# A third weight slot, deeper norm buffers, ScalarE stores and a one-piece RWKV recurrence with four-tile updates

## What is computed

```python
def _wkv_step(S, inp):
    r_t, w_t, k_t, v_t, a_t, b_t = inp
    sa = jnp.einsum('zbhvk,zbhk->zbhv', S, a_t)
    S = S * w_t[..., None, :] + sa[..., :, None] * b_t[..., None, :] + v_t[..., :, None] * k_t[..., None, :]
    return S, jnp.einsum('zbhvk,zbhk->zbhv', S, r_t)
...
    def expert_block(args):
        xb, e = args
        return (jax.nn.silu(xb @ w_gate[e]) * (xb @ w_up[e])) @ w_down[e]
...
        hl2 = rmsnorm(x, norm2_g[i]) * (1 + sc2) + sh2
```

## Time and profile before

| | us |
|---|---|
| median of 3 runs | 4429.95 |
| profiled execution | 4436.23 |
| its span | 4434.4 |
| gMLP mixer | 0 to 657 |
| norm, routing, experts of layer 0 | 671 to 1334 |
| recurrence with its preparation | 1816 to 2725 |
| norm, routing, experts of layer 1 | 2839 to 3482 |
| rest of the layers | to 4434 |

### The profile page before, as it was taken

How to read it: one execution, slowest core, us unless ns; L and a number is a source line. 1 busy time by engine, 2 the same in 40 slices (tenths; PEclk the granted TensorE clock), 3 DMA queues, 4 the chain that set the end, 5 groups by cost and what they waited for, 6 DMA issues and landing times. The chain is left out here.

```text
span 4434.4 us, 104053 instructions
## 1 busy us (share of the span) xinstructions
PE 3704.5 (84%) x46088; PEld 2369.3 (53%) x46088; DVE 1252.4 (28%) x2933; ACT 775.7 (17%) x1775; POOL 620.5 (14%) x794
## 2 busy tenths in 40 slices
PE   4999995999992399688888886789999469997887
PEld 2445544555551145477777784456565234664464
DVE  2140114111110620245555554421111120331153
ACT  1011001000000100233433331100000010321142
POOL 0000000211110100244444430011111100000000
PEclk7999996999996599799999997789999779658988
DMA  7731105999996512100000003479999732101000
GB/s 277 286 146 38 72 19 193 394 396 384 388 392 222 130 69 76 50 15 17 18 18 18 17 6 112 145 284 397 392 388 386 257 98 90 38 1 63 24 39 24
DMA packets 303038, 707.10 MB, mean 159 GB/s; under 512 B 26829, under 2 KB 50349, under 8 KB 301964
## 3 DMA queue, kind: packets, MB, share of 16 engines
q1 hardware_dynamic: 268036, 613.55, 37.5%
q0 software_dynamic: 25840, 71.67, 4.8%
q10 hardware_dynamic: 8728, 15.34, 0.9%
HBM read 648.20 MB, written 52.31 MB: 158 GB/s over the span
## 5 line engine op out<-in xcount | busy, mean ns | idle before, releaser
L901 PE MATMUL banks<-w_gate_up_ring,x_turned 128*32 128x256 f32 x12288 | 695.3, 382 | 33.4 <-DMA w_gate_up_ring<-in_moe_w_up_dram 31.9
L901 PEld LDWEIGHTS banks<-w_gate_up_ring,x_turned 128*32 128x32 f32 x12288 | 425.8, 110 | 275.6 <-issue 56.6
L919 PE MATMUL banks<-w_down_ring,hidden_turned 128*32 128x256 f32 x6144 | 344.8, 380 | 0.0
L878 POOL DMA_DIRECT2D y_rows<-y_out_rows x256 | 142.0, 562 | 946.1 <-ACT y_out_rows L963 910.9
L977 DVE TENSOR_TENSOR hidden<-silu_gate,banks 128x128 f32<-128x128 f32 x192 | 55.3, 288 | 770.1 <-ACT silu_gate L957 770.1
L337 PE MATMUL banks<-const_cols,h_tokens 128*128 128x128 f32 x240 | 55.1, 411 | 250.0 <-DVE h_tokens L310 163.2
L919 PEld LDWEIGHTS banks<-w_down_ring,hidden_turned 128*32 128x32 f32 x6144 | 193.1, 110 | 128.6
L1914 DVE TENSOR_TENSOR inverse_both_ways<-banks,inverse_both_ways 128x512 f32<-128x512 f32 (+1 forms) x240 | 152.2, 637 | 253.2 <-PE banks L1823 252.3
L866 POOL DMA_INDIRECT x_rows<-h_rows,cell_index x64 | 62.9, 983 | 921.0 <-POOLq L42 895.4
L456 PE MATMUL banks<-gmlp_weights,h_turned_gmlp 128*128 128x512 f32 x384 | 174.7, 610 | 12.3 <-DMA gmlp_weights<-in_ga_w_in_dram 12.3
L337 PEld LDWEIGHTS banks<-const_cols,h_tokens 128*128 128x128 f32 x240 | 46.4, 220 | 259.5 <-DVE h_tokens L310 170.8
(11 more groups left out here) (456 smaller groups left out, 5475.4 us busy)
## 6 DMA issues: line engine op xcount, KB each, us to landing
w_gate_up_ring<-in_moe_w_gate_dram SPq DMA_DIRECT2D x70, 2048.0 KB, 19.8
w_gate_up_ring<-in_moe_w_up_dram SPq DMA_DIRECT2D x70, 2048.0 KB, 24.0
w_down_ring<-in_moe_w_down_dram SPq DMA_DIRECT2D x70, 2048.0 KB, 21.6
u_channels<-in_ada_w_dram SPq DMA_DIRECT2D x40, 1024.0 KB, 6.8
y_rows<-y_out_rows POOLq DMA_DIRECT2D x256, 96.0 KB, 5.3
gmlp_weights<-in_ga_w_in_dram SPq DMA_DIRECT2D x8, 2048.0 KB, 8.2
ab_weights<-in_ab_w_in_dram SPq DMA_DIRECT2D x6, 2048.0 KB, 8.7
ada_first<-in_ada_w_dram SPq DMA_DIRECT2D x2, 4096.0 KB, 17.4
```

What stands on the lines that cost most here:

```text
L878: pool.dma_start(y_blocks[e, j], ys[strip(j), r, :, :]).then_inc(y_out[r], 16)
L901: last = pe.matmul(ps[strip(j), GU + g, 0:2 * FQ].rearrange("p (a c) -> p a c", a=2), xT[:, e % 2, k, strip(g)], wgu[:, e % 2, :, k, j * F ...
L919: last = pe.matmul(ps[strip(j), Y + g // 2, (g % 2) * DQ:(g % 2 + 1) * DQ], hT[:, g, strip(k)], wd[:, e % 2, k, j * DQ:(j + 1) * DQ], star ...
```

## The change

Four things. (1) In the norms ahead of the experts `h_tokens` has five buffers; the squares use the last of them; SP waits for the stores at the norm's end, no longer in `route`. (2) Gate/up has a third slot, allocated once the norm's memory is free. Its first load is issued by SP in `route`'s block; expert e uses slot e % 3, and is asked for when expert e − 3 has done its gate/up. Down keeps two slots. (3) The four y stores of an expert are issued by ACT behind its own copy of y. (4) `recurrence` is one block: 24 rounds in a row with semaphores counted over all of them; the constants' load, the first preparation and the last scan are in it as well. P1 is split in XM (at the head) and RB (beside level 1). XA and XM are laid over a kept identity `XI` by `copy_predicated` on DVE; ACT copies the rows L; POOL makes LQ of all levels only. The updates of a level, MV and WU use all four quarters of the array, TA, TB, TK and MV stand inside the levels, WU is moved out half by ACT and half by DVE, F by ACT and its identity by POOL. Lora sums go one at a time through bank 7, the norm's transposes in two halves.

```diff
+        deep = 2 if keep is None else KEPT
+        h = sb("h_tokens", [P, deep, D])
...
+                    if j >= deep:
+                        dve.wait_ge(turned, 2 * (j - deep + 1))
                         if keep is not None:
-                            dve.wait_ge(kept[j % 2], 16 * (j // 2))
+                            dve.wait_ge(kept[j % deep], 16 * (j // deep))
                     g, s = place[name(gains[j])], shifts[j]
-                    op = dve.scalar_tensor_tensor(h[:, j % 2, :], core.x[:, t, :], rs[:, j:j + 1], spread[:, g, :], ALU.mult, ALU.mult)
...
-        wgu = sb("w_gate_up_ring", [P, 2, 2, KD, F])
+        wgu = [sb(f"w_gate_up{r}", [P, 2, KD, F]) for r in range(2)]
...
+        def load_third(sp):
+
+            sp.dma_start(wgu[2][:, 0, :, :], gate_src[2]).then_inc(gu_in[2], 16)
+            sp.dma_start(wgu[2][:, 1, :, :], up_src[2]).then_inc(gu_in[2], 16)
...
+                      [mod_row(core, layer, t >= NT, 3) for t in range(nt)], 1e-6, hT, keep=(h_rows, kept), loads=loads, router=(wr, router_in))
+        wgu.append(sb("w_gate_up2", [P, 2, KD, F]))
+        route(core, layer, nt, nb, br, weights, index, home, beyond, load_third)
+        experts(core, layer, h_rows, y_rows, index, wgu, wd, gate_src, up_src, down_src, gu_in, down_in, beyond, xb, next_gu, next_d)
...
                 for e in range(2, E):
                     r = e % 2
-                    sp.wait_ge(gu_sum, GROUPS * (e - 1))
-                    sp.dma_start(wgu[:, r, 0, :, :], gate_src[e]).then_inc(gate_in[r], 16)
-                    sp.dma_start(wgu[:, r, 1, :, :], up_src[e]).then_inc(up_in[r], 16)
+                    if e > 2:
+                        sp.wait_ge(gu_sum, GROUPS * (e - 2))
+                        sp.dma_start(wgu[e % 3][:, 0, :, :], gate_src[e]).then_inc(gu_in[e % 3], 16)
+                        sp.dma_start(wgu[e % 3][:, 1, :, :], up_src[e]).then_inc(gu_in[e % 3], 16)
                     sp.wait_ge(y_sum, 2 * (e - 1))
                     sp.dma_start(wd[:, r, :, :], down_src[e]).then_inc(down_in[r], 16)
                 first = sp.value_load(beyond[0:1, 1:2], min_val=0, max_val=E - 1)
...
                     if e >= 2:
-                        act.wait_ge(y_out[e % 2], 16 * QUARTERS * (e // 2))
+                        act.wait_ge(y_stored[e % 2], 16 * QUARTERS * (e // 2))
                     act.activation(ys[:, e % 2, 2, :], ps[:, Y + 1, 0:DQ], ACT.Copy).then_inc(y_high, 1)
+                    act.wait_ge(y_low, e + 1)
+                    act.wait_ge(y_high, e + 1)
+                    for j in range(QUARTERS):
+                        act.dma_start(y_blocks[e, j], ys[strip(j), e % 2, :, :]).then_inc(y_stored[e % 2], 16)
+                for r in range(2):
+                    act.wait_ge(y_stored[r], 16 * QUARTERS * E // 2)
 
...
+                part = slice(z * LORA, (z + 1) * LORA)
+                for half in range(2):
+                    done = 4 * n + 2 * z + half
+                    if done:
+                        self.wait(pe, "sig_done", done)
+                    pe.matmul(ps[:, 7, 0:H2], w[part, :], src[part, half * H2:(half + 1) * H2], start=True, stop=True).then_inc(s["lora_sum"], 1)
+                    yield
...
+        to_row = lambda h, cc: row[cc ^ h]
+        from_row = lambda h, cc: row[cc ^ h ^ 1]
...
+        rounds = [(c, rnd, pair) for c in range(KD) for rnd, pair in enumerate(PAIRS)]
...
+                sp.dma_start(con[:, :], ins["scan_const"]).then_inc(const_in, 16)
+                prepare[0].load(sp, products, 0)
+                for c in range(KD):
+                    if c + 1 < KD:
+                        prepare[c + 1].load(sp, products, PE.of("F", 3 * (c - 1) + 2) if c else 0)
+                    if c:
+                        scan[c - 1].store(sp)
+                scan[KD - 1].store(sp)
+                scan[KD - 1].wait(sp, "y_stored", 16)
...
                     for n in lv:
+                        X = XI if n == 1 else XX
+                        for h in range(2):
+                            wait(by_dve, DVE, f"XA_{h}" if n == 1 else f"XX{n - 1}_{h}")
+                            wait(by_pool, POOL, f"LQ{n}_{h}")
+                            for u in range(4):
+                                for cc in range(2):
+                                    last = pe.matmul(ps[from_row(h, cc), 4 * h + 1, u * CHUNK:(u + 1) * CHUNK], LQ[h][to_row(h, cc), n - 1, u, :],
+                                                     X[h][to_row(h, cc), 0, u, :], start=True, stop=True)
+                            PE.mark(last, products, f"Z{n}_{h}")
...
+                                wait(by_dve, DVE, f"XM_{h}")
+                            wait(by_act, ACTS, f"Z{n}_{h}")
...
-                            if n < LEVELS - 1:
-                                for u in range(4):
-                                    for cc in range(2):
-                                        pe.matmul(ps[row[cc], 4 * h, u * CHUNK:(u + 1) * CHUNK], XX[h][row[cc], 1, u, :], Z[h][row[cc], u, :], start=True, stop=True)
-                            for u in range(4):
-                                for cc in range(2):
-                                    last = pe.matmul(ps[row[cc], 4 * h, (4 + u) * CHUNK:(5 + u) * CHUNK], Z[h][row[cc], u, :], XX[h][row[cc], 1, u, :], start=True, stop=True)
+                                    here = from_row(h, cc)
+                                    if n < last_lv:
+                                        pe.matmul(ps[to_row(h, cc), 4 * h, u * CHUNK:(u + 1) * CHUNK], X[h][here, 1, u, :], Z[h][here, u, :], start=True, stop=True)
+                                    last = pe.matmul(ps[here, 4 * h + 1, (4 + u) * CHUNK:(5 + u) * CHUNK], Z[h][here, u, :], X[h][here, 1, u, :], start=True, stop=True)
                             PE.mark(last, products, f"XX{n}_{h}")
...
+                        wait(by_dve, DVE, f"XX{last_lv}_{h}")
+                    wait(by_act, ACTS, "MV")
+                    for u in range(4):
+                        for h, cc in quads:
+                            here = from_row(h, cc)
+                            last = pe.matmul(ps[row[cc], 4 * h + 1, u * P:(u + 1) * P], XX[h][here, 1, u, :],
+                                             AM[h][here, u, :, :].rearrange("p a c -> p (a c)"), start=True, stop=True)
+                    PE.mark(last, products, "WU")
...
+                    wait(by_act, ACTS, "WU_0")
+                    wait(by_dve, DVE, "WU_1")
...
+                        dve.wait_ge(products, PE.of("XA", R))
+                        DVE.mark(dve.copy_predicated(by_dir(XI[h][:, 0, :, :]), both("x0", 2, CHUNK).bitcast(U32), by_dir(fours(ps[:, 4 * h + 1, low]))),
                                  by_dve, f"XA_{h}")
                     for h in range(2):
-                        dve.wait_ge(products, PE.of("P2", rnd))
+                        dve.wait_ge(by_act, ACTS.of(f"L_{h}", R))
+                        DVE.mark(dve.copy_predicated(by_dir(XI[h][:, 1, :, :]), both("q1_0", 2, CHUNK).bitcast(U32), by_dir(fours(ps[:, 4 * h, low]))),
...
+                    need("XM")
                     for h in range(2):
-                        last = copy(AM[h][:, :, 0, :], ps[:, 0, :].rearrange("p (u h c) -> p u h c", u=4, h=2)[:, :, h, :])
-                    ACTS.mark(last, by_act, "TA")
-                    need("TB")
-                    ACTS.mark(copy(Bk[:, :, :].rearrange("p u c -> p (u c)"), ps[:, 4, :]), by_act, "TB")
-                    for h in range(2):
-                        need(f"MV_{h}")
-                        ACTS.mark(copy(AM[h][:, :, 1, :], fours(ps[:, 4 * h + 2, 0:4 * CHUNK])), by_act, f"MV_{h}")
+                        if R:
+                            act.wait_ge(by_pool, POOL.of(f"LQ{last_lv}_{h}", R - 1))
+                        for cc in range(2):
+                            last = copy(L[h][row[1 - cc], :, :], fours(ps[row[cc], 4 * h, low]))
+                        ACTS.mark(last, by_act, f"L_{h}")
...
+                    need("WU")
+                    ACTS.mark(copy(WU[:, :, :, 0, :], ps[:, 1, :].rearrange("p (u a c) -> p u a c", u=4, a=2)), by_act, "WU_0")
...
+                def whole_factor(R):
+                    c, rnd, pair = rounds[R]
+                    pool.wait_ge(by_act, ACTS.of("F", R))
+                    at = outs[c % 2]["F"][:, :, 2 * pair[0]:2 * pair[1] + 2, :]
+                    pool.tensor_tensor(at, at, c_("ident64").unsqueeze(1).unsqueeze(1).to_broadcast([P, DIRS, 4, CHUNK]), ALU.add).then_inc(f_whole, 1)
```

995 lines of the change are left out of this document (495 added, 500 removed).

## The result

The changed kernel takes 4380.23 us, the median of 4 runs (4376.56 to 4380.42), against 4430.03 for the kernel before in the same job: a ratio of 0.9884 (95% interval 0.9866 to 0.9901), 50 us faster. Forecast were 196 us. The profiled executions are 4376.56 and 4436.23 us, 59.7 apart. The table puts that down to stages, each measured between two rows of the timeline of PE that both kernels have.

The account below looks back on a forecast made before the run. PE was taken to bound the recurrence, with PE and DMA nearly level in the experts. 4436 less 172 (recurrence) and 24 (experts, norms, stores) gave 4240, put 6.3 lower for the median: 4234 us, range 4165 to 4340.

Parts of the forecast that it names:

- Tiles: Recurrence: level updates, MV and WU take about half the time on four array tiles; 16.1 us per block of two heads.
- Moved work: Recurrence: kept identity, WU evacuated by two engines and no idle block end save 4.0, 0.9 and 3.9 us per block.
- given back as waits: Recurrence: late hand-overs stop PE, 2.0 us at round heads and 1.2 for preparing the next heads, per block.
- rival (a): Recurrence: hand-offs eat the four-tile saving, levels stay near 3.5 us, only borders and round heads are won; 4336 us, chance 0.17.
- copy_predicated: Recurrence, four a round on DVE: taken at 0.415 us each, bounds 0.2 and 0.83; the upper would cost 20 us.
- DVE's 128x512 add: Recurrence, in the chain through one head of a level: estimated at about 0.7 us.
- Third slot: Expert loops: gate/up weights asked for earlier, so the queue never runs dry; 9 us in layer 0, 7 in layer 1.
- Norm: Norm ahead of layer 0's experts: five buffers remove DVE's waits for stores of h rows; 6.5 us.
- y stores: Expert loops: with ACT issuing, the last stores go out 0.5 us earlier per layer; 1 us.
- (b): Experts and recurrence: weights come at PE's floor and a steady block is five us shorter than forecast; 4170 us, chance 0.15.
- (c): Recurrence: the four tiles don't overlap in this order, so 129 us less is won; 4334 us, chance 0.05.
- (d): Experts: ACT's store issues block and delay the next expert's rows; slower than before from 2.4 us an issue, chance 0.04.

Follow-up runs that it names:

- two_tiles: The changed kernel with level updates, MV and WU put back on two tiles of the array; 4449.69 us, ratio 1.0064 to the kernel before.
- burst2: The changed kernel plus 1024 products of 64x64 in a row ahead of the recurrence, on two quarters of the array; the row took 61.5 us.
- burst4: The changed kernel plus 1024 products of 64x64 in a row ahead of the recurrence, on all four quarters of the array; the row took 59.0 us.
- warm0: The changed kernel plus eight unread 128x128 products behind level 1 in round 0 of each block of two heads; 4361.85 us, one run.
- best1: The changed kernel with the scan's state cleared earlier, 4 filler products before P2 each round and 6 behind level 1 of round 0; 4340.10 us, ratio 0.9792.
- rec_only: The kernel before with only the new recurrence; 4399.11 us, ratio 0.9952.
- moe_only: The changed kernel with the old recurrence; 4399.76 us, ratio 0.9955.
- warm: The changed kernel plus unread 128x128 products before later levels' updates in rounds 1 and 2, and before WU and Q in all; 4414.39 us, ratio 0.9983.

## Why the prediction was right in sign and wrong in size

The bound was read right: PE in the recurrence, DMA and PE level in the experts. The terms:

**Tiles, 129 forecast: right as work, spent before it reached the time.** Updates, MV and WU halved as read from L1780's 0.64 us, and two_tiles gives 124 us of PE's work at full clock. The step that failed is the one from busy time to time. The sum priced a run of matmuls by L1780, 32 of them, with their loads a quarter of the 256 instructions of a block, and took it to hold for thousands. Two costs stood against it that the sum did not have:

- *Instruction blocks: 54 us* (64.1 against 10.4 of "issue"). The trace of before had such standstills already, 14 of them, and I did not read them; with slower matmuls on two tiles most of the blocks' time is covered, as in burst2. The Trainium skill, "Runtime: NRT & Kernel Launch", Instruction fetch mechanics, says that PE's instructions come in 16 KiB blocks of 256 and that crossing a block is mostly hidden; burst4 agrees with the size and shows the crossing not hidden once a block is done in 2.10 us.
- *The clock: about 40 us of busy time* (90 us more at the lower level, PE busy in nine tenths of it). The sum took every duration from rows at full clock. Before, most low spells last 3.4 to 4 us, about half of them at the borders; after, they reach 27.5 us (in the window at 0.69) and begin in or behind a block's head. That most of it comes back when PE has work at that place is shown by warm0 (0.96, one run) and best1 (0.98, 4 runs), each with more work for PE and less time. What starts a spell stays open.

Two more terms were short by 17 us: of the tiles' 129 us 124 came, and the new structure has some 15 us more work for PE at full clock where R·B's 3 were counted. These figures lean on a mean clock of two digits and can be off by some 4 us each.

**Moved work, 67 forecast less 30 given back as waits: 37, measured 14.** That is for the same window, from the first XA to the last F: eight times 4.9 us and seven borders of 3.9, less 3.2 in each of six blocks and some 10 in the first and the last. Idle time other than "issue" went from 102.3 to 88.6 us. The borders went as forecast (35.4 of PEq's 37.9 us). But POOL's identity was only replaced by POOL's LQ (24.6 to 17.4), WU's wait did not shorten (11.2 to 14.3: two half evacuations of 0.69 us start at the same time, and DVE's is late), two waits are new, 16.0 for ACT's step and 18.0 ahead of the norm's transposes (L1437), whose halves go through one bank, and that for the state grew from 7.5 to 9.9. So 53 us were given back where 30 were counted. This is rival (a) in part: hand-offs cost 23 us more, not 129. Its mark, Z waiting in every level for DVE's add, is not there, and the levels did shrink.

These make up the gap: 54 + 40 + 17 + 23 are 134 of the 141 us missing between the first XA and the last F, and some 6 more lie in gaps too short for the view of the waits. At the recurrence's start and end 2.9 us were won where 9 were forecast; no run takes these 6 apart.

**copy_predicated**, taken at 0.415 between 0.2 and 0.83, costs 0.448. **DVE's 128x512 add**, estimated at 0.7, takes 0.69. Both right.

**Third slot, 16 forecast, 1.5 measured.** The lower end of that term, 7 us a layer, failed too. Its bytes were right: the third slot is full when expert 0 starts, and the stream starts some 5 us later behind it, as counted. The step that failed held the rate. Its 384 GB/s came from a count of 210 MB; the view gives 390 for these 547 us, and 387 from the stream's start (766.80) to expert 31 in after, in layer 1 389 and 385. That is 4 to 6 us a layer. How far one profile can be trusted here: in rec_only, with the experts of before, the loops took 560.7 and 560.5 us, in moe_only, with those of after, 558.6 and 560.0. So the gain is some 2 us in layer 0, and in layer 1 it is lost in a scatter of 3. PE still waits 29.9 us for up weights, with fewer and longer waits. Why three slots lower the rate is open: POOL's or ACT's stores make no difference, and reordering SP's queue made it worse.

**Norm, 6.5 forecast, 3.9 measured.** PE is next, as forecast, but its router matmuls (6.88 us for the last two tiles) end the block. Routing starts at 712.66 us, before the 714 forecast, but by luck: 3.8 us of that were won ahead of the norm.

**y stores, 1 forecast, 8 measured.** I priced the issue of four stores and left out what waits behind POOL's last ones at the loop's end.

**Rivals (b), (c), (d)** fell: experts still wait, updates take 0.6 us a head, and ACT's store issues take 0.45 us in the median and 1.67 at most, far from the 2.4 that would have decided.

Of the marks given for a right forecast, the updates' time and the vanished border came; a steady block of 83 us did not (93.1), nor did the 17.8 us period of an expert.

## What to carry to other kernels

Count instructions as well as busy time before a step is sped up: in these runs 128 matmuls of PE with their loads did not pass faster than about 3.7 us in a long row, so that quarter-array tiles paid only where waits or larger matmuls stood between them. When a faster engine brings its waits together at one place, look at the granted clock of the stretch behind that place, and price it at the lower level too. Where an engine is made the faster, a few matmuls of no use at the point where it stands still can win time, as in best1; at other places they cost time, as in warm.

## What the runs showed of the chip that was not expected

- 256 PE instructions of 64x64 products take about as long on four quarters of the array as on two (59.0 and 61.5 us for 4096), with 1.4 to 1.9 us of standstill at each block on four and none on two.
- A wait of 8.9 us ahead of the burst bought 150 matmuls without a standstill, hardly more than one block.
- A float32 product of 64x64 by 64 columns, and one of 128x128 by 128, is two weight loads and two matmuls in the records (1024 products, 2048 matmuls; 240 fillers, 480).
- 64 four-column products a round went with a clock of 0.84 instead of 0.89 to 0.91, with PE busy 84% of the time; eight full-size products in one round of three went with 0.96 (one run each).
- With the DMA engines at a share of 1.04 throughout, the rate was 391, 388 and 384 GB/s with two slots, with three, and with the third asked for still earlier; it was 387 with three slots and POOL's stores.
